# GpSimd issues the additions of an expert block ahead of the gathers for the block four later

## The chip, the core and the metric

The kernel runs on one core of a Trainium2 chip. The metric is the device time in microseconds (us) of one execution. The core's engines run on their own and meet at semaphores: PE (TensorE), DVE (VectorE), ACT (ScalarE), POOL (GpSimd) and SP (SyncE, which here only issues transfers). Sixteen DMA engines move data between the memory and the core for all of them.

## What is computed

One decoder layer on 1040 rows of 1024 numbers (16 meta tokens and 1024 tokens): an RG-LRU mixer, a layer norm, a mixture of experts, a layer norm. The change lies in the routed experts. Each row picks 8 of 64 experts; the reference gathers the rows of a block, runs one expert on them, weights the result and adds it to the rows that it came from:

```python
    def body(b, acc):
        rows = lax.dynamic_slice(row_tok, (b * EXPERT_BLOCK,), (EXPERT_BLOCK,))
        rw = lax.dynamic_slice(row_w, (b * EXPERT_BLOCK,), (EXPERT_BLOCK,))
        e = block_e[b]
        gu = x_pad[rows] @ w_gu[e]
        y = ((jax.nn.silu(gu[:, :f]) * gu[:, f:]) @ w_down[e]) * rw[:, None]
        return acc.at[rows].add(y)
```

A shared expert on all rows and the second layer norm follow.

## The kernel before

**Blocks.** Experts are sorted by the number of their rows. The kernel walks through 64 blocks in this execution, block t for one expert. Even blocks hold 164 rows, odd ones 128. A hardware loop runs 30 times over a pair (an even and an odd block), and four blocks follow it unrolled. `t = i + j` is the block, `b = j % 2` its parity, and every buffer of a block exists twice, one for each parity.

**What a block needs, engine by engine**, each engine in the order of its own program:

- SP loads the weights of the expert: two transfers of 1 MB (`wgu`, three blocks ahead) and one of 1 MB (`wd_raw`, two ahead).
- GpSimd issues the gathers, transfers that fetch rows by an index list: six of 128 KB for an even block, four for an odd one (`fetch`, L843), from `h1_rows` into `xg[b]`. It also issues the additions, transfers that add the block's result to `routed_rows` row by row (L874): two for an even block (128 and 36 rows), one for an odd one. All of them go through one software DMA queue.
- DVE in its step t: `wd_lo` of block t (L1414); `turn(t+2)`, which waits for the gathers of block t+2 and transposes `xg` into `xT` (L1372); `rows_from(t+4)`, the index list for the gathers of block t+4 (L1351); `hidden(t+1)` (L1382 to L1390); then the wait on `ysb_free`; `rows_of(t)`, which looks up the target rows and weights of block t (`picks`, L1357, to `to_row`, L1367) and stands right ahead of y; and its share of `y(t)`, the weighted result in `ysb[b]` (L1430, L1434).
- ACT in its step t: `wd_hi` of block t (L1136), the two `silu` of block t+1 (L1125), the wait on `ysb_free` and on `rows_of(t)`, and its share of `y(t)` (L1145, L1149).
- PE: `up(t+1)` (L996, needs `turn(t+1)`), then `down(t)` (L121 to L123, L1021, L1023; needs `wd_lo(t)` and `hidden(t)`).

**The order on GpSimd**, which the change touches. In its step t GpSimd first waits until `turn(t+2)` is done (`xT_ready`, so that `xg[b]` is free), waits for `rows_from(t+4)` inside `fetch`, and issues the gathers of block t+4. Then it waits until the additions of block t-1 have landed (`y_stored`), raises `ysb_free` (L868), which lets DVE and ACT make `y(t+1)`, waits for the two shares of `y(t)` (`y_act`, `y_dve`) and issues the additions of block t. Blocks 0 to 3 are gathered ahead of the loop.

Of the kernel before, what the change touches and what calls it, by code (L numbers as in the profile page):

```python
# [125 lines left out]
def build(nc, hT, h_rows, w_in, chan, w_gates, w_out, ln, router_w, router_b, w_gu, w_down,  # L126
# [534 lines left out]
    xg_clear, xT_ready = sem("xg_clear"), sem("xT_ready")  # L661
# [4 lines left out]
    def before(counts, i, j):  # L666


        return i * (sum(counts) // 2) + j // 2 * sum(counts) + j % 2 * counts[0]

    def stores_to(i, j):

        return loads(i, j) * STORES[j % 2] + 16 * (j % 2)
# [35 lines left out]
    sp_pass, pool_pass, pe_pass = sem("sp_pass"), sem("pool_pass"), sem("pe_pass")  # L709
# [13 lines left out]
    def steps(eng):  # L723

        n = eng.value_load(sched_i[0:1, 5:6], min_val=E - 4, max_val=T_MAX - 4)
        with eng.Fori(0, n, 2) as i:
            for b in range(2):
                yield i, b, 4
        for j in range(4):
            yield n, j, 3 - j  # L730

    with nc.Block() as block:  # L732
# [72 lines left out]
        @block.gpsimd  # L805
        def _(pool):

            s = Chain(pool, pool_step)
            s.n = pool_steps
            pool.memset(h1T[:, :, L:LP], 0.0).then_inc(z_clear, 1)  # L810
            pool.wait_ge(list_cleared, 16)

            def enlist(i):

                r = ROWS[i]
                pool.wait_ge(place_ready, i + 1)
                for j in range(TOP_K):
                    pool.indirect_dma_start(  # L818
                        out=expert_list,
                        out_offset=bass.IndirectOffsetOnAxis(ap=place[0:r, i, j:j + 1], axis=0),  # L820
                        in_=entry[0:r, i, j, :], in_offset=None).then_inc(listed, 16)

            for i in range(TILES - 2):
                enlist(i)

            pool.wait_ge(z_lo_ready, AHEAD + TILES)
            pool.wait_ge(norm_ready, TILES)
            for b in range(2):
                pool.memset(hid_hi[b][:, :, :].bitcast(F32), 0.0).then_inc(hid_clear, 1)
                pool.memset(hid_lo[b][:, :, :].bitcast(F32), 0.0).then_inc(hid_clear, 1)  # L830
                pool.memset(xg[b][:, :, :], 0.0).then_inc(xg_clear, 1)
            for i in range(TILES - 2, TILES):
                enlist(i)
            pool_n[0] = s.n


            def fetch(i, j):

                b = j % 2
                pool.wait_ge(from_ready, i + j + 1)  # L840
                pool.sem_inc(pool_pass, 1)
                for g in range(GB[b]):
                    pool.indirect_dma_start(  # L843
                        out=xg[b][:, g, :], out_offset=None, in_=h1_quarters,
                        in_offset=bass.IndirectOffsetOnAxis(ap=from_row[b][:, g:g + 1], axis=0),
                        bounds_check=NQ * L - 1, oob_is_err=False).then_inc(gathered[b], 16)

            pool.wait_ge(routed_cleared, 16)
            pool.wait_ge(routed_begun, 16 * TILES)
            pool.wait_ge(h1_stored, 16 * TILES)  # L850
            pool.wait_ge(xg_clear, 2)
            fetch(0, 0)
            fetch(0, 1)
            for j in range(2, 4):
                pool.wait_ge(xT_ready, j - 1)
                fetch(0, j)
            pool.wait_ge(sched_loaded, 16)
            for i, j, more in steps(pool):
                t, b = i + j, j % 2
                if more >= 4:  # L860
                    pool.wait_ge(xT_ready, t + 3)
                    pool.sem_inc(pool_pass, 1)
                    fetch(i, j + 4)

                pool.wait_ge(y_stored[1 - b], stores_to(i, j - 1))
                pool.sem_inc(ysb_free, 1)  # L868
                pool.wait_ge(y_act, t + 2)
                pool.sem_inc(pool_pass, 1)  # L870
                pool.wait_ge(y_dve, YS[1] + before(YS, i, j + 1))
                pool.sem_inc(pool_pass, 1)
                for half, r in enumerate((P, REST[b])[0:STORES[b]]):
                    pool.indirect_dma_start(  # L874
                        out=routed_rows,
                        out_offset=bass.IndirectOffsetOnAxis(ap=to_row[b][0:r, half:half + 1],
                                                             axis=0),
                        in_=ysb[b][0:r, half, :], in_offset=None,
                        bounds_check=L - 1, oob_is_err=False, compute_op=ALU.add
                        ).then_inc(y_stored[b], 16)  # L880

        @block.tensor
        def _(pe):
# [671 lines left out]
```

## Time and profile before

| | us |
|---|---|
| median of 3 runs | 1330.15 (1327.42 to 1332.71) |
| the profiled execution, its own time | 1323.39 |
| its span, first to last instruction | 1321.6 |
| PE busy in the span | 1223.2 (93%) |
| DVE busy | 825.8 (62%) |
| POOL busy | 661.9 (50%) |
| ACT busy | 431.8 (33%) |

A busy time is the sum of what an engine's instructions took, waits left out. The loop over the blocks fills the time from about 478 to 1270 us of the span; the mixer and the routing stand ahead of it, the last layer norm behind it. The median of the runs is 6.76 us above the profiled execution, whose rows are read below.

### The profile page before, as it was taken

The page shows a single profiled execution, that of the slowest core. Times are in us where ns is not written, and L with a number is a line of the kernel's source. Part 1 is how long each engine was busy: PE and PEld are TensorE (multiplying, and loading weights), DVE is VectorE, ACT ScalarE, POOL GpSimd, SP SyncE. Part 2 cuts the span into 40 slices and gives each one's busy share as a digit, 9 for nine tenths or more (in the row PEclk, how much of TensorE's full clock was granted, in tenths as well). Part 3 has the DMA queues.
Part 4 walks back from the last instruction along what each step waited for, and adds up shares of the span by engine and source line. Part 5 has one row for each costly group of instructions (what it writes and reads, how often), then busy time and mean ns, then how long its engine had stood idle before and what let it go on. Part 6 is the DMA issues. An engine that isn't in the chain of part 4 may idle for free. (4 is left out here: it accounts for less than half of the span.)

```text
span 1321.6 us, 23551 instructions
## 1 busy us (share of the span) xinstructions
PE 1223.2 (93%) x7492; PEld 1102.0 (83%) x7492; DVE 825.8 (62%) x1685; ACT 431.8 (33%) x597; POOL 661.9 (50%) x556
## 2 busy tenths in 40 slices
PE   7999999669898989999999999999999999999974
PEld 7999999647686668998899997999999899999831
DVE  7474839376887616655666664666566566656538
ACT  5352542713333012332333232333223332333223
POOL 6222211220665555665676667656666766657310
PEclk9999999889999989999999999999999999999987
DMA  7111110323242389999999999999999999999754
GB/s 274 49 48 33 48 49 17 127 76 125 97 130 70 97 247 382 363 346 358 350 344 371 350 356 317 347 342 359 340 350 359 314 370 345 318 376 334 225 127 170
DMA packets 86406, 320.39 MB, mean 242 GB/s; under 512 B 18144, under 2 KB 34581, under 8 KB 61409
## 3 DMA queue, kind: packets, MB, share of 16 engines
q1 hardware_dynamic: 56991, 250.68, 49.8%
q0 software_dynamic: 29072, 68.82, 21.1%
q10 hardware_dynamic: 306, 0.40, 0.1%
q8 instruction: 23, 0.38, 0.1%
q14 instruction: 14, 0.11, 0.0%
HBM read 278.71 MB, written 53.16 MB: 251 GB/s over the span
## 5 line engine op out<-in xcount | busy, mean ns | idle before, releaser
L996 PEld LDWEIGHTS bank<-xT,wgu 128*128 128x128 f32 x4096 | 524.4, 192 | 22.8 <-issue 15.3
L996 PE MATMUL bank<-xT,wgu 128*128 128x164 f32 (+1 forms) x4096 | 531.1, 290 | 11.7 <-issue 5.6
L843 POOL DMA_INDIRECT xg<-h_rows,from_row x320 | 353.4, 1104 | 123.3 <-issue 96.7
L874 POOL DMA_INDIRECT routed_rows<-ysb,to_row x96 | 150.9, 1572 | 190.6 <-issue 184.4
L1145 ACT ACTIVATE ysb<-bank,of_row 128x512 f32<-128x512 f32 x64 | 44.0, 687 | 418.9 <-issue 219.2
L1414 DVE TENSOR_TENSOR wd_lo<-wd_raw,wd_hi 128x1024 fp32r<-128x1024 f32 x128 | 151.2, 1223 | 43.9 <-ACT wd_hi L1136 21.6
L121 PE MATMUL bank<-hT_hi,win_hi 128*128 128x348 f32 x384 | 124.2, 324 | 9.6 <-DVE hT_lo L556 9.6
L1136 ACT ACTIVATE wd_hi<-wd_raw 128x1024 fp32r<-128x1024 f32 x128 | 127.9, 1048 | 1.4 <-issue 0.6
L122 PE MATMUL bank<-hT_lo,win_hi 128*128 128x348 f32 x384 | 124.0, 323 | 0.0
L123 PE MATMUL bank<-hT_hi,win_lo 128*128 128x348 f32 x384 | 123.5, 322 | 0.0
L818 POOL DMA_INDIRECT expert_list<-entry,place x72 | 74.2, 1030 | 89.7 <-DVE place L1253 69.9
L121 PE MATMUL bank<-wd_hi,hid_hi 128*128 128x512 f32 x256 | 108.2, 423 | 10.0 <-DVE wd_lo L1414 9.2
L369 POOL TENSOR_TENSOR win_lo<-win_raw,win_hi 128x1024 fp32r<-128x1024 f32 x16 | 40.9, 2559 | 147.8 <-ACT win_hi L473 147.8
L1372 DVE STREAM_TRANSPOSE xT<-xg 128x1536 f32<-128x1536 f32 x64 | 96.4, 1506 | 25.6 <-DMA xg<-h_rows,from_row 25.6
L122 PE MATMUL bank<-wd_lo,hid_hi 128*128 128x512 f32 x256 | 101.8, 398 | 0.6 <-issue 0.6
L123 PE MATMUL bank<-wd_hi,hid_lo 128*128 128x512 f32 x256 | 101.9, 398 | 0.2 <-issue 0.2
L1357 DVE TENSOR_TENSOR picks<-lists,pick 128x24 f32<-128x24 f32 x64 | 12.2, 190 | 134.0 <-POOLq L868 101.0
L121 PE MATMUL bank<-wout_hi,z_hi 128*128 128x512 f32 x144 | 61.3, 425 | 24.0 <-DVE z_lo L1163 12.6
L121 PEld LDWEIGHTS bank<-hT_hi,win_hi 128*128 128x128 f32 x384 | 72.8, 189 | 9.6 <-issue 9.6
L1125 ACT ACTIVATE gact<-bank 128x128 f32<-128x128 f32 (+1 forms) x128 | 34.8, 289 | 130.9 <-PE bank L996 86.1
L1382 DVE TENSOR_TENSOR hid<-gact,bank 128x128 f32<-128x128 f32 (+1 forms) x128 | 38.5, 301 | 55.8 <-PE bank L996 30.6
L122 PEld LDWEIGHTS bank<-hT_lo,win_hi 128*128 128x128 f32 x384 | 72.7, 189 | 0.0
(221 smaller groups left out, 1774.5 us busy)
## 6 DMA issues: line engine op xcount, KB each, us to landing
wgu<-in_w_gu SPq DMA_DIRECT2D x128, 1024.0 KB
wd_raw<-in_w_down SPq DMA_DIRECT2D x64, 1024.0 KB
win_raw<-in_w_in SPq DMA_DIRECT2D x16, 512.0 KB, 3.9
xg<-h_rows,from_row POOLq DMA_INDIRECT x320
hT_raw<-in_hT SPq DMA_DIRECT2D x8, 520.0 KB, 7.8
wout_raw<-in_w_out SPq DMA_DIRECT2D x1, 4096.0 KB, 12.8
h_in<-in_h_rows SPq DMA_DIRECT2D x8, 512.0 KB
h_rows<-h SPq DMA_DIRECT2D x8, 512.0 KB
```

The source lines that it names most:

```text
L121: pe.matmul(out, lhs[0], rhs[0], start=first, stop=False)
L122: pe.matmul(out, lhs[0], rhs[1], start=False, stop=False)
L123: return pe.matmul(out, lhs[1], rhs[0], start=False, stop=last)
L369: pool.tensor_tensor(win_lo[q % NW][:, :, :], win_raw[q % NW][:, :, :], win_hi[q % NW][:, :, :].bitcast(F32), ALU.subtract).then_inc(win_l ...
L818: pool.indirect_dma_start(out=expert_list, out_offset=bass.IndirectOffsetOnAxis(ap=place[0:r, i, j:j + 1], axis=0), in_=entry[0:r, i, j, : ...
L843: pool.indirect_dma_start(out=xg[b][:, g, :], out_offset=None, in_=h1_quarters, in_offset=bass.IndirectOffsetOnAxis(ap=from_row[b][:, g:g ...
L874: pool.indirect_dma_start(out=routed_rows, out_offset=bass.IndirectOffsetOnAxis(ap=to_row[b][0:r, half:half + 1], axis=0), in_=ysb[b][0:r, ...
L996: mm = pe.matmul(bank[:, 2 * f + half, 0:BLOCK[b]], wgu[b][:, f, k, c:c + P], xT[b][:, k, 0:BLOCK[b]], start=(k == 0), stop=(k == KT - 1))
L1136: act.activation(wd_hi[b][:, k, :], wd_raw[b][:, k, :], ACT.Copy).then_inc(wd_hi_ready, 1)
L1145: act.activation(ysb[b][:, 0, 0:512], bank[:, 4, :], ACT.Copy, scale=of_row[b][:, 0, 1:2]).then_inc(y_act, 1)
L1372: dve.transpose(xT[b][:, :, :].rearrange("p k (g a) -> p k g a", a=SQ), xg[b][:, :, :].rearrange("p g (k c) -> p k g c", c=SQ)).then_inc(x ...
L1414: dve.tensor_tensor(wd_lo[b][:, k, :], wd_raw[b][:, k, :], wd_hi[b][:, k, :].bitcast(F32), ALU.subtract).then_inc(wd_lo_ready, 1)
```

## The change

In GpSimd's step the lines that gather block t+4 move from the top of the step to its end. Nothing is added or removed; the waits inside the moved lines go along with them.

```diff
             for i, j, more in steps(pool):
                 t, b = i + j, j % 2
-                if more >= 4:
-                    pool.wait_ge(xT_ready, t + 3)
-                    pool.sem_inc(pool_pass, 1)
-                    fetch(i, j + 4)
                 pool.wait_ge(y_stored[1 - b], stores_to(i, j - 1))
                 pool.sem_inc(ysb_free, 1)
...
                         ).then_inc(y_stored[b], 16)
+                if more >= 4:
+                    pool.wait_ge(xT_ready, t + 3)
+                    pool.sem_inc(pool_pass, 1)
+                    fetch(i, j + 4)
```

## Rows read from the trace of the kernel before

**Rows 1.** Windows: busy us of each engine, granted clock, DMA share, GB/s.
```profile
478.00:1260.00 782.00, 762.94 (x5110) 708.52 (x5111) 475.13 (x1017) 240.56 (x383) 491.28 (x405) 0.99 1.00 341
```

**Rows 2.** Waits of DVE, 520 to 1250 us: total us, times, longest.
```profile
DVE picks L1357 <- POOLq L868: 98.3, 25, 7.2
...
DVE xT L1372 <- DMA xg<-h_rows,from_row: 5.8, 8, 1.1
```

**Rows 3.** Timeline of PE: start, us, line, operation, tiles, count, [idle before].
```profile
528.81 1.42 PE L996 MATMUL bank<-xT,wgu 128*128 128x164 f32 x9
...
552.32 0.86 PE L996 MATMUL bank<-xT,wgu 128*128 128x164 f32 x5
```

**Rows 4.** Timeline of DVE: turn(38), last of hidden(37), look-up of block 36.
```profile
935.36 1.77 DVE L1372 STREAM_TRANSPOSE xT<-xg 128x1536 f32<-128x1536 f32 x1
...
938.39 0.29 DVE L1387 TENSOR_TENSOR hid_lo<-hid,hid_hi 128x128 fp32r<-128x128 f32 x1
943.21 0.20 DVE L1357 TENSOR_TENSOR picks<-lists,pick 128x24 f32<-128x24 f32 x1 [4.53 <-POOLq L868]
```

**Rows 5.** Timeline of DVE: look-up and y of block 0, then turn(4).
```profile
505.79 0.20 DVE L1357 TENSOR_TENSOR picks<-lists,pick 128x24 f32<-128x24 f32 x1 [0.64 <-issue]
...
508.01 1.40 DVE L1434 SCALAR_TENSOR_TENSOR ysb<-bank,of_row,y_rest 36x512 f32<-36x512 f32 x2 [0.93 <-ACT y_rest L1149]
...
522.29 1.76 DVE L1372 STREAM_TRANSPOSE xT<-xg 128x1536 f32<-128x1536 f32 x1
```

**Rows 6.** Timeline of DVE: the end of y(26).
```profile
828.24 1.40 DVE L1434 SCALAR_TENSOR_TENSOR ysb<-bank,of_row,y_rest 36x512 f32<-36x512 f32 x2 [0.63 <-ACT y_rest L1149]
```

**Rows 7.** Timeline of POOL: the first addition of block 26.
```profile
830.52 2.09 POOL L874 DMA_INDIRECT routed_rows<-ysb,to_row  x1 [4.80 <-DVE ysb L1434]
```

**Rows 8.** Timeline of POOL: first and last gather of block 40, both additions of 36.
```profile
945.28 1.04 POOL L843 DMA_INDIRECT xg<-h_rows,from_row  x1 [0.30 <-issue]
...
952.11 1.00 POOL L843 DMA_INDIRECT xg<-h_rows,from_row  x1 [0.30 <-issue]
954.73 1.62 POOL L874 DMA_INDIRECT routed_rows<-ysb,to_row  x1 [1.62 <-issue]
956.66 1.44 POOL L874 DMA_INDIRECT routed_rows<-ysb,to_row  x1 [0.30 <-issue]
```

**Rows 9.** Timeline of POOL: the last gather of block 0, of block 8, of block 60.
```profile
473.80 1.01 POOL L843 DMA_INDIRECT xg<-h_rows,from_row  x1 [0.30 <-issue]
...
561.79 1.00 POOL L843 DMA_INDIRECT xg<-h_rows,from_row  x1 [0.30 <-issue]
...
1194.88 1.00 POOL L843 DMA_INDIRECT xg<-h_rows,from_row  x1 [0.30 <-issue]
```

**Rows 10.** Timeline of DVE: turn(0), turn(8), turn(60), turn(62).
```profile
476.03 1.78 DVE L1372 STREAM_TRANSPOSE xT<-xg 128x1536 f32<-128x1536 f32 x1 [9.15 <-DMA xg<-h_rows,from_row]
...
569.83 1.78 DVE L1372 STREAM_TRANSPOSE xT<-xg 128x1536 f32<-128x1536 f32 x1 [1.03 <-DMA xg<-h_rows,from_row]
...
1201.28 1.77 DVE L1372 STREAM_TRANSPOSE xT<-xg 128x1536 f32<-128x1536 f32 x1
...
1224.30 1.77 DVE L1372 STREAM_TRANSPOSE xT<-xg 128x1536 f32<-128x1536 f32 x1
```

**Rows 11.** Timeline of PE: up(62), then the first matmul of down(61) and of down(63).
```profile
1230.07 9.07 PE L996 MATMUL bank<-xT,wgu 128*128 128x164 f32 x64
1240.04 0.47 PE L121 MATMUL bank<-wd_hi,hid_hi 128*128 128x512 f32 x1 [0.90 <-DVE wd_lo L1414]
...
1259.29 0.77 PE L121 MATMUL bank<-wd_hi,hid_hi 128*128 128x512 f32 x1 [4.20 <-DVE wd_lo L1414]
```

**Rows 12.** Timeline of DVE: the end of y(62).
```profile
1256.16 1.40 DVE L1434 SCALAR_TENSOR_TENSOR ysb<-bank,of_row,y_rest 36x512 f32<-36x512 f32 x2 [0.91 <-ACT y_rest L1149]
```

**Rows 13.** Timeline of POOL: the first addition of block 62, the addition of block 63.
```profile
1261.19 1.56 POOL L874 DMA_INDIRECT routed_rows<-ysb,to_row  x1 [5.50 <-issue]
...
1268.82 1.57 POOL L874 DMA_INDIRECT routed_rows<-ysb,to_row  x1 [4.34 <-issue]
```

## The prediction

> **What bounds the kernel now.** I read the windows over the block loop first. From 478 to 1260 us PE is busy for 762.94 of 782.00 us at a granted clock of 0.99, and the DMA engines are busy all the time (share 1.00) [rows 1]. So PE has 19 us to win in the whole loop, and no more. Then PE's timeline: from the start of up(4) to the start of up(6) it needs 23.51 us for a pair of blocks without a gap [rows 3]. The loop as a whole takes a little more: turn(4) starts at 522.29 and turn(62) at 1224.30, which is 702.01 us for 29 pairs, 24.21 each [rows 5, 10]. PE and the DMA engines set the pace together, and the rest of the loop follows about as fast.
>
> Next I looked for who is late, in the waits of DVE. The largest is the look-up of a block waiting for GpSimd's release of ysb (L868): 98.3 us in 25 waits, up to 7.2 [rows 2]. The change takes hold right there: GpSimd issues six gathers for about 8 us [rows 8] and only then releases ysb. A reader who stops here expects a gain. But this wait ends on DVE, and PE has hardly an idle slot behind it; and the same view has a second row that matters more: eight times a turn waited for its gathers, 5.8 us in all [rows 2]. Those gathers were issued early, by the order which the change gives up. So I followed the gathers.
>
> **The change, part by part.** *Number of instructions.* None is added or removed. GpSimd already alternates additions and gathers; what changes is which gathers stand between two groups of additions. Before: additions of t-1, gathers of t+4, additions of t. After: additions of t-1, gathers of t+3, additions of t. The work of GpSimd for a pair is the same. What it is moved past: the wait for the landing of the additions of t-1, the release of ysb, and the waits for y(t). In the software DMA queue each group of gathers moves behind the additions of one more block. The queue of SP is not touched.
>
> *What the release of ysb gains: nothing that lasts.* The release for y(t+1) now stands behind the gathers of t+3 instead of those of t+4, again one group of gathers behind the additions of t-1, whose landing it waits for in any case. I put it at 0.
>
> *What the gathers lose.* This is the term. After the change the gathers of t+4 can't be issued before the additions of t, these not before y(t), and y(t) stands on DVE behind turn(t+2) in the same step. And turn(t+2) waits for the gathers of t+2. That closes a ring over one pair of blocks: landing of the gathers of t+2, turn(t+2), hidden(t+1), look-up and y(t), additions of t, gathers of t+4, their landing. Before, the gathers of t+4 only had to come behind the additions of t-1 and so y(t-1) and turn(t+1): the same ring had three blocks of time instead of two. I add the ring up for even t, which has more gathers and more additions:
>
> - turn(t+2) and hidden(t+1), from the start of the turn at 935.36 to the end of the last hidden instruction at 938.39 + 0.29: 3.32 us [rows 4].
> - The pause until the look-up begins where nothing holds it up: 0.64 [rows 5]. (In rows 4 it was 4.53, held by L868; in the ring ysb is free by then, since GpSimd stands waiting for y(t) behind its release.)
> - Look-up and y(t), 505.79 to 508.01 + 1.40: 3.62 [rows 5].
> - From the end of y to the first addition where GpSimd waits for it: 828.24 + 1.40 = 829.64 to 830.52, 0.88 [rows 6, 7].
> - Two additions, 954.73 to 956.66 + 1.44: 3.37, and 0.30 to the next instruction [rows 8].
> - Six gathers, 945.28 to 952.11 + 1.00: 7.83 [rows 8].
>
> The sum is 19.96 us without the landing of the last gather. The trace shows a landing only where a turn waits for it: block 8's came 569.83 - 562.79 = 7.04 us after the last issue ended, with the weights streaming beside it; block 0's came 476.03 - 474.81 = 1.22 us after it, ahead of the loop [rows 9, 10]. Where a turn didn't wait there is an upper bound: block 60's rows were there 1201.28 - 1195.88 = 5.40 us after [rows 9, 10]. So the bounds are 1.2 and 7.0. Most turns of the loop did not wait, so I take a value near the row of block 60, 5.6: a little above it, because the gathers now stand right behind two additions in their queue, and well below 7.0, because a slower loop asks less of the DMA engines. The ring is then 19.96 + 5.6 = 25.56 us, above PE's 23.51 and above today's 24.21. For odd t the ring has one addition less (954.73 to 956.66: 1.93 us) and two gathers less (a fifth of 945.28 to 952.11 each: 2.7 us), so it is shorter by over 4 us and does not bind [rows 8].
>
> The Trainium skill, "DMA: Bandwidth & Descriptors", section on the anatomy of one DMA on the SWDGE path, gives a fixed 2.0 us plus the bytes over 436 GB/s for a transfer issued by GpSimd; my estimate from it is 2.3 us for a gather of 128 KB. The trace agrees for block 0 (1.22 us, even less) and disagrees for block 8 (7.04 us). By the page the ring would be 22.3 us and would not bind at all.
>
> *The sum.* y(0) ends at 508.01 + 1.40 = 509.41 [rows 5]. The additions and gathers behind it and the landing take 0.88 + 3.37 + 0.30 + 7.83 + 5.6 = 17.98, so turn(4) starts at 527.4 instead of 522.29. 29 rings of 25.56 are 741.2 us, so turn(62) starts at 1268.6 instead of 1224.30 [rows 10]. Before, up(62) began at 1230.07, 4.0 us after that turn had ended at 1226.07 [rows 10, 11]; now PE waits at that place, so up(62) begins as the turn ends, at 1270.4: 40.3 us later. Behind it something is given back, since GpSimd is no longer late: the first addition of block 62 came 3.63 us after the end of y(62) (1257.56 to 1261.19), where 0.88 is needed, and PE's wait of 0.90 us ahead of down(61) goes too [rows 11 to 13]. That is 2.75 + 0.90 = 3.6 us. The change is +36.7 us. The profiled execution took 1323.39 us and would take 1360.1; on the median, 1330.15 + 36.7 = 1366.9, rounded to 1367.
>
> Each tenth of a microsecond of landing time is worth 3 us (30 landings on the way: those of blocks 4 to 62).
>
> *What PE's waits may add.* PE now waits 25.56 - 23.51 = 2.05 us in each pair, ahead of an even up. After a wait of 0.90 us the first matmul of a down took 0.47 us, after one of 4.20 us it took 0.77 [rows 11], so matmuls may run slower behind a long wait. A wait of 2 us lies between, and PE has those 2 us to spare for a slower stretch; I put it at 0 and keep it for the upper end.
>
> **Rivals.**
>
> *Faster: the gathers land early enough, and the earlier additions win.* If the ring falls under 24.2 us, GpSimd's old lateness (98.3 us of waits) can shrink, and PE's idle 19 us go at best: 1330 - 19 = 1311. The point is a mean landing time of 4.2 us (19.96 + 4.2 = 24.2). For it speaks that the ring itself thins the traffic and that idle engines landed a gather in 1.22 us; against it that DMA is busy for the whole loop and that eight turns waited even with gathers issued a block earlier. This is where the page's rule would lead.
>
> *No change: the landing takes about 4.2 to 4.6 us*, and the ring costs what today's lateness costs: 1330 within 7.
>
> *Much slower: the gathers queue behind the additions*, and the landing is block 8's 7.0 us or more: 1.4 us more for each of 30 landings is 42 us, so 1409 and above. Matmuls that run slower behind PE's waits would lead there too.
>
> *The change does nothing*, since GpSimd alternates anyway: that is the case of no change, and the shift by one block speaks against it.
>
> **Chances.** The forecast, a landing time of about 4.7 to 6.9 us, 1340 to 1406: 0.70. Faster 0.08. No change 0.12. Much slower 0.10. The predicted time is the forecast's, 1367. The range takes in half of the two neighbours: 1330 to 1412. A measurement of this kernel can tell about 0.5% (6.7 us) from no change: faster by more than that 0.08, within it 0.12, slower 0.80.
>
> **What would show it.** In the profile of the changed kernel: the starts of even turns stand about 25.6 us apart; even turns wait for the DMA of xg nearly every time, several us each, where eight waits of 1.1 at most stood; PE idles about 2 us in a pair ahead of an even up; the look-up no longer waits for L868 ahead of even blocks; GpSimd's first addition of an even block waits for DVE's y (L1434), not for issue. I am wrong if even turns don't wait for xg, or if GpSimd's additions still wait for the landing of the ones before. If turns wait but the pair takes under 24.5, the landing time was mis-sized.

## The result, and the profile after

The changed kernel takes 1416.64 us (median of 4 runs, 1414.59 to 1423.69), the kernel before 1331.43 beside it: 1.065 times as long, 95% interval 1.060 to 1.070, 85 us more. Forecast were 1367 us, with a range up to 1412. The sign and the ring came true, the size did not: 37 us were forecast. The profiled execution took 1415.9 us, its span 1414.1, against 1323.39 and 1321.6 before.

First the window over the block loop, 478 to 1352 us (columns: stretch, length, busy us and instructions of PE, weight loads, DVE, ACT, POOL, then granted clock, DMA share, GB/s), which answers [rows 1]:

```profile
478.00:1352.00 874.00, 798.48 (x5130) 732.99 (x5128) 478.13 (x1018) 245.33 (x383) 501.06 (x411) 0.97 0.93 306
```

PE is now idle for 76 us of the loop (874.00 - 798.48), and the DMA engines, busy throughout before, are idle for 7% of it on average. Neither sets the pace any more. Who does is in the waits, 520 to 1340 us (who waited for whom: us in total, times, longest):

```profile
ACT ysb L1144 <- DVE to_row L1366: 304.4, 44, 13.6
POOL routed_rows L869 <- DVE ysb L1433: 227.7, 31, 21.4
DVE xT L1371 <- DMA xg<-h_rows,from_row: 203.6, 31, 10.5
...
PE bank L995 <- DVE hid_lo L1386: 37.2, 9, 5.4
```

The look-up's wait for the release of ysb, the largest of DVE in [rows 2], is gone. In its place stands what the forecast named: the even turns wait for their gathers, all 30 of them and one odd turn, 203.6 us in 31 waits where [rows 2] had 5.8 in 8, and GpSimd waits for y, not y for GpSimd.

The ring can be read off one pair. Here it is for DVE, from turn(6) to turn(8), and for GpSimd between them (start, length; the wait ahead in brackets):

```profile
568.58 1.78 DVE L1371 STREAM_TRANSPOSE xT<-xg 128x1536 f32<-128x1536 f32 x1 [10.13 <-DMA xg<-h_rows,from_row]
...
571.62 0.29 DVE L1386 TENSOR_TENSOR hid_lo<-hid,hid_hi 128x128 fp32r<-128x128 f32 x1
572.55 0.20 DVE L1356 TENSOR_TENSOR picks<-lists,pick 128x24 f32<-128x24 f32 x1 [0.64 <-issue]
...
574.77 1.40 DVE L1433 SCALAR_TENSOR_TENSOR ysb<-bank,of_row,y_rest 36x512 f32<-36x512 f32 x2 [0.92 <-ACT y_rest L1148]
...
594.43 1.78 DVE L1371 STREAM_TRANSPOSE xT<-xg 128x1536 f32<-128x1536 f32 x1 [6.16 <-DMA xg<-h_rows,from_row]
```

```profile
577.05 2.09 POOL L869 DMA_INDIRECT routed_rows<-ysb,to_row  x1 [7.18 <-DVE ysb L1433]
579.45 1.44 POOL L869 DMA_INDIRECT routed_rows<-ysb,to_row  x1 [0.30 <-issue]
581.19 1.09 POOL L843 DMA_INDIRECT xg<-h_rows,from_row  x1 [0.30 <-issue]
...
588.32 1.00 POOL L843 DMA_INDIRECT xg<-h_rows,from_row  x1 [0.30 <-issue]
```

Turn and hidden 3.33 (to 571.91), pause 0.64, look-up and y 3.62 (to 576.17), 0.88 to the first addition, two additions 3.84 (to 580.89), 0.30, six gathers 8.13 (to 589.32), landing 5.11: 25.85 us, with nothing left over. That is near the forecast of 25.56. But the mean is not: turn(4) starts at 538.01 and turn(62) at 1322.58, 784.57 us for 29 pairs, 27.05 each, where [rows 5, 10] gave 24.21.

The whole difference of the two spans, 92.5 us, divides so: 6.3 us before turn(0), where nothing was changed (482.4 against [rows 10]); 9.4 from turn(0) to turn(4) (forecast 5.1); 82.6 in the 29 pairs (forecast 39.2); and 5.8 given back behind turn(62) (forecast 7.6: the slack of 4.0 and the tail of 3.6). In a second profile of the changed kernel, turn(0) starts at 476.67, turn(4) at 529.61 and turn(62) at 1315.0, so turn(0) comes 0.6 us later than before, the stretch from turn(0) to turn(4) is 6.7 us longer, and the pair takes 27.08. The miss is the pair, in both.

### The profile page after: what moved, and what is told of

Read it like the earlier page. It is cut to its first block and busy times, and to the rows that moved or that the text cites. A ratio compares the mean times of both kernels' runs of the same rounds, so it can differ in the third digit from the quotient of the medians.

```text
span 1414.1 us, 23551 instructions
## 1 busy us (share of the span) xinstructions
PE 1262.2 (89%) x7492; PEld 1130.7 (80%) x7492; DVE 828.1 (59%) x1685; ACT 436.5 (31%) x597; POOL 667.0 (47%) x556
## 5 line engine op out<-in xcount | busy, mean ns | idle before, releaser
L995 PE MATMUL bank<-xT,wgu 128*128 128x164 f32 (+1 forms) x4096 | 559.5, 297 | 67.6 <-DVE hid_lo L1386 37.2
L995 PEld LDWEIGHTS bank<-xT,wgu 128*128 128x128 f32 x4096 | 546.0, 197 | 87.2 <-DVE hid_lo L1386 41.4
L843 POOL DMA_INDIRECT xg<-h_rows,from_row x320 | 344.5, 1077 | 110.8 <-issue 96.7
L869 POOL DMA_INDIRECT routed_rows<-ysb,to_row x96 | 164.9, 1718 | 281.0 <-DVE ysb L1433 235.5
L123 PEld LDWEIGHTS bank<-hT_hi,win_lo 128*128 128x128 f32 x384 | 72.9, 190 | 0.0
```

The source lines that it names most:

```text
L123: return pe.matmul(out, lhs[1], rhs[0], start=False, stop=last)
L843: pool.indirect_dma_start(out=xg[b][:, g, :], out_offset=None, in_=h1_quarters, in_offset=bass.IndirectOffsetOnAxis(ap=from_row[b][:, g:g ...
L869: pool.indirect_dma_start(out=routed_rows, out_offset=bass.IndirectOffsetOnAxis(ap=to_row[b][0:r, half:half + 1], axis=0), in_=ysb[b][0:r, ...
L995: mm = pe.matmul(bank[:, 2 * f + half, 0:BLOCK[b]], wgu[b][:, f, k, c:c + P], xT[b][:, k, 0:BLOCK[b]], start=(k == 0), stop=(k == KT - 1))
```

## The experiments

The theory (the ring): the pace is the sum of the steps from one even turn's gathers to the next, and whatever stands in that chain costs its own length in each of 29 pairs. The rivals: the order in the software queue (gathers behind additions land late), and throughput (PE, DVE or the DMA engines are simply slower, and the wait for the gathers only shows it).

### How many gathers stand behind the additions

Four kernels issue the first gathers of block t+4 at the top of the step, as before, and the others behind the additions, as in the change. `first` is (1, 0), (2, 1), (3, 2) and (4, 3) for even and odd blocks; the kernel before is (6, 4), the changed one (0, 0). `fetch` takes the slice of the gathers to issue as a third argument, which isn't shown.

```diff
+                first = (1, 0)[b]
+                if more >= 4 and first:
+                    pool.wait_ge(xT_ready, t + 3)
+                    pool.sem_inc(pool_pass, 1)
+                    fetch(i, j + 4, slice(None, first))
...
                         ).then_inc(y_stored[b], 16)
+                if more >= 4:
+                    if not first:
+                        pool.wait_ge(xT_ready, t + 3)
+                        pool.sem_inc(pool_pass, 1)
+                    fetch(i, j + 4, slice(first or None, None))
```

Expected of (1, 0):

> One of the six gathers of an even block goes ahead of the additions (odd block: none), the rest stay behind them. Ring theory (gathers of t+4 behind y(t) behind turn(t+2) behind gathers of t+2): a pair took 27.05 us in the changed kernel, and each gather that goes ahead takes its 8.29 / 6 = 1.38 us out of the ring, so 25.7 a pair and 1417 - 29 x 1.38 = 1377 us. Queue theory (gathers land late because they stand behind additions in the DMA queue): the loss of 85 us goes with the share of gathers that stand behind, 9 of 10, so about 1408 us.

Of (2, 1):

> Two of the six gathers of an even block and one of four of an odd block go ahead of the additions. Ring theory: 27.05 - 2 x 1.38 = 24.3 us a pair, about what the kernel before takes (24.2), so about 1335 us. Queue theory: 7 of 10 gathers still stand behind additions, 1331 + 0.7 x 85 = 1391 us.

Of (3, 2):

> Three of six and two of four gathers go ahead of the additions. Ring theory: the ring is 22.9 us and binds no more; the time is that of the kernel before, 1331, or up to 10 us less, since ysb is released behind five gathers instead of six ahead of an even block. Queue theory: half of the gathers stand behind additions, 1331 + 0.5 x 85 = 1374 us.

Of (4, 3):

> Four of six and three of four gathers ahead of the additions, two and one behind. Ring theory: the ring is 21.5 us and is far from binding, so the time is that of the run with three and two ahead, 0.994 of the kernel before, within 0.4%. Queue theory: a third of the gathers still behind additions, slower than the kernel before by 25 us.

| ahead | us | ratio to before (95%) | turn(4), turn(62) | us per pair |
|---|---|---|---|---|
| 0, 0 (the change) | 1416.64 | 1.065 (1.060 to 1.070) | 538.0, 1322.6 | 27.05 |
| 1, 0 | 1365.67 | 1.026 (1.021 to 1.030) | 534.8, 1272.6 | 25.44 |
| 2, 1 | 1342.90 | 1.006 (1.001 to 1.012) | 534.5, 1243.6 | 24.45 |
| 3, 2 | 1324.35 | 0.994 (0.992 to 0.997) | 530.1, 1229.8 | 24.13 |
| 4, 3 | 1331.25 | 0.999 (0.996 to 1.003) | 527.1, 1238.1 | 24.52 |
| 6, 4 (before) | 1331 | 1 | 522.3, 1224.3 | 24.21 |

One even gather taken out of the chain (1.00 + 0.30 us) takes 1.6 us off the pair, the second 1.0, the third 0.3 (with the second and the third, an odd gather moves too). So the curve falls as the ring says and flattens where the ring comes down to the other bound. The queue rival in the form that was forecast, a loss in proportion to the gathers behind additions, is out: it wanted 1408, 1391 and 1374 us for the first three. With (3, 2) the kernel is 0.6% faster than before, by one comparison; with (4, 3) there is no difference. The last was forecast at 0.994 within 0.4%: a small miss.

The waits of (3, 2), 520 to 1250 us:

```profile
POOL routed_rows L873 <- issue: 157.8, 87, 7.9
DVE xT L1376 <- DMA xg<-h_rows,from_row: 154.2, 57, 5.9
```

GpSimd's waits are no longer put down to y, and the turns wait briefly, even and odd (57 times, 2.7 us on average where the changed kernel has 6.6). PE is busy for 717.50 us of that window, at a granted clock of 1.00.

### The same order, written in another place

The program order of before, gathers at the top of the step, but for block t+3: the gathers then stand behind the same additions as in the change, in another place of the loop's text.

```diff
-            for j in range(2, 4):
+            for j in range(2, 3):
...
-                if more >= 4:
-                    pool.wait_ge(xT_ready, t + 3)
+                if more >= 3:
+                    pool.wait_ge(xT_ready, t + 2)
                     pool.sem_inc(pool_pass, 1)
-                    fetch(i, j + 4)
+                    fetch(i, j + 3)
```

> The program order of the kernel before, gathers at the top of the step, but for the block three later instead of four, so that GpSimd issues the same sequence of gathers and additions as the changed kernel. Ring theory: only the distance counts, so about 1417 us, the time of the changed kernel. Place theory (the loss comes from where the release of ysb and the waits for y stand in the step): about 1331 us, the time of the kernel before.

Measured: 1412.72 us, ratio 1.060 (1.055 to 1.065), turn(4) at 529.0 and turn(62) at 1322.4, 27.36 a pair. That is the changed kernel's time, as it should be: but for the ends of the loop, GpSimd runs the same instructions and waits in the same order in both. So where the lines stand in the step is nothing, only the order counts. What it is about the order that costs, the ring or the place in the queue, this run can't tell; the others do.

### Delays on GpSimd, inside and outside the ring

First, four register reads between the additions and the gathers of even blocks, and the same reads ahead of the wait for y, where GpSimd is idle.

```diff
                         ).then_inc(y_stored[b], 16)
+                for _ in range(0 if b else 4):
+                    blocks_to_run(pool)
                 if more >= 4:
```

> The changed kernel, and for even blocks GpSimd reads a register from the schedule four times between the additions and the gathers behind them, some 1.5 to 3 us in which it issues nothing. Ring theory: this stands in the ring, so each us costs 29 us, 44 to 87 in all: 1460 to 1504. Throughput theory (GpSimd has too much to do in a pair): the same.

> The changed kernel, and the same four reads for even blocks between the release of ysb and the wait for y, where GpSimd waited for y 7.3 us on average (227.7 us in 31 waits). Ring theory: they disappear in that wait, 1417 us within 7. Throughput theory: GpSimd has as much to do as with the reads behind the additions, so 1460 to 1504.

Measured: 1388.67 us (1.048, 1.044 to 1.052) and 1391.67 (1.051, 1.047 to 1.055). No difference, and the first is no test, since the reads did not delay the gathers, where 1.5 to 3 us had been expected. The gap behind the additions stayed what it was (909.65 to 909.96), 0.31 us on average over 29 pairs. Both ratios are also 0.014 to 0.017 below the changed kernel's 1.065, which was not forecast; it comes up again below.

```profile
908.21 1.44 POOL L869 DMA_INDIRECT routed_rows<-ysb,to_row  x1 [0.30 <-issue]
909.96 1.08 POOL L843 DMA_INDIRECT xg<-h_rows,from_row  x1 [0.30 <-issue]
```

Then eight short fills of an unused tile (`scratch`, with a semaphore of its own) on GpSimd in the same two places, in every block.

```diff
+                pool.wait_ge(scratch_done, t * 8 + 1)
+                pool.sem_inc(pool_pass, 1)
+                for n in range(8):
+                    pool.memset(scratch[:, n, :], 0.0).then_inc(scratch_done, 1)
```

> The changed kernel with eight short memsets of unused space on GpSimd between the additions and the gathers of every block, about 0.15 us each with the pause behind it, 1.2 us in all. (Register reads in this place, tried before, ran on beside the additions and held nothing up.) Ring theory: 1.2 us more in the ring of even blocks, 29 x 1.2 = 35 us above the changed kernel. Throughput theory (GpSimd's work of a pair sets the pace): 29 x 2.4 = 70 us above.

> The same eight memsets behind the release of ysb, ahead of the wait for y. Ring theory: ahead of an even block they run while GpSimd waits for y anyway, so within 7 us of the changed kernel. Throughput theory: 70 us above it, as in the run with the memsets behind the additions.

Beside them, the changed kernel once more:

> The changed kernel once more, on the chip on which the next runs are timed: as before 1.050 to 1.065 of the kernel before.

Measured: 1401.66 (1.048, 1.040 to 1.056), 1398.22 (1.050, 1.044 to 1.055), and the changed kernel 1412.40 (1.060, 1.053 to 1.067). The fills took 1.03 us, but began beside the second addition, which ends at 949.53:

```profile
948.10 1.43 POOL L872 DMA_INDIRECT routed_rows<-ysb,to_row  x1 [0.30 <-issue]
949.05 1.03 POOL L882 MEMSET scratch<- 128x30 f32 x8
950.24 1.08 POOL L845 DMA_INDIRECT xg<-h_rows,from_row  x1 [0.16 <-issue]
```

The gap grew from 0.30 to 0.71, so the ring would ask for 0.41 x 29 = 12 us; 3 us more by the medians and 2 less by the ratios were measured against the same fills outside the ring, which can't be told from 0 or from 12. They rule out only that GpSimd's throughput is the bound: then both would have come out slower than the changed kernel, and both came out a little faster.

### Delays on DVE, inside and outside the ring

DVE's rows stand one behind the other, so a delay can't hide here: 24 fills of such a tile ahead of the look-up of even blocks (in the ring), and of odd blocks (outside; there `b == 1`).

```diff
                 dve.wait_ge(ysb_free, t + 1)
                 dve.sem_inc(dve_pass, 1)
+                if b == 0:
+                    dve.wait_ge(scratch_done, t * 12 + 1)
+                    for n in range(24):
+                        dve.memset(scratch[:, n, :], 0.0).then_inc(scratch_done, 1)
                 rows_of(i, j)
```

> The changed kernel with 24 short fills of an unused tile on DVE, ahead of the look-up of every even block (about 0.07 us each by the fill of the tile small in the profile, so 1.6 us by estimate). These stand in the ring: behind hidden(t+1), ahead of the look-up and y(t). The ring theory: every pair is longer by what they take, 29 x 1.6 = 46 us over the kernel with the same fills ahead of odd blocks. The rival, that the pace is set by the DMA queue or by PE's slower stretches and the gathers only seem to be a chain: DVE is idle for almost half of the time, so the same time as with the fills ahead of odd blocks, within 10 us.

> The same fills ahead of the look-up of every odd block, which the ring does not bind. The ring theory: odd blocks have about 4 us to spare (one addition and two gathers less), so the time of the changed kernel (ratio 1.05 to 1.065) within 10 us, and some 46 us less than with the fills ahead of even blocks. The rival (DVE's or PE's time is what counts): the same time as with the fills ahead of even blocks.

Measured: 1436.91 us (1.082, 1.076 to 1.088) in the ring, 1387.40 (1.045, 1.040 to 1.050) outside it. From the trace of the first:

```profile
947.22 0.29 DVE L1388 TENSOR_TENSOR hid_lo<-hid,hid_hi 128x128 fp32r<-128x128 f32 x1
947.46 0.71 DVE L1433 MEMSET scratch<- 128x10 f32 x24
948.90 0.20 DVE L1358 TENSOR_TENSOR picks<-lists,pick 128x24 f32<-128x24 f32 x1 [0.73 <-issue]
```

The fills were shorter than estimated: the pause of 0.64 us became 1.39 (947.51 to 948.90), 0.75 more, so the ring asks for 22 us over the changed kernel. Against the changed kernel's ratios of 1.060 and 1.065 the difference is 0.017 to 0.022 of 1331, 22 to 29 us. The profiled execution, the fastest of the four, shows less: 27.42 us a pair, 0.35 over the changed kernel's two profiles, so 10 us: the pause is 0.75 us longer in every pair, but the other terms of the ring came out 0.4 shorter in sum. The same work on the same engine, one block later, made nothing slower. DVE's throughput is out, and the fills count in the ring and not outside it.

Not expected was that the fills outside made the kernel faster than the changed one, by 1.5 to 2%. Its pairs took 25.66 us (turn(4) 536.5, turn(62) 1280.6). Of the 49 us between the two kernels the fills in the ring explain 22 at most; the others are this gain.

### Time taken out of the ring

The wait for ysb and the look-up of even blocks move ahead of turn(t+2), into the time when DVE waits for the gathers.

```diff
+                if b == 0:
+                    dve.wait_ge(ysb_free, t + 1)
+                    dve.sem_inc(dve_pass, 1)
+                    rows_of(i, j)
                 if more >= 2:
                     dve.wait_ge(up_done, t * UPS + 2 * UPS)
                     turn(i, j + 2)
...
-                dve.wait_ge(ysb_free, t + 1)
-                dve.sem_inc(dve_pass, 1)
-                rows_of(i, j)
+                if b == 1:
+                    dve.wait_ge(ysb_free, t + 1)
+                    dve.sem_inc(dve_pass, 1)
+                    rows_of(i, j)
```

> The changed kernel with the wait for ysb and the look-up of even blocks moved ahead of turn(t+2), where DVE waits for the gathers anyway. It takes the pause of 0.64 us and the look-up out of the ring, and ACT's share of y can run beside hidden(t+1): from the end of hidden to the end of y about 2.5 us in the place of 4.3. The ring theory: 1.8 us less in each pair, 29 x 1.8 = 52 us less than the changed kernel, ratio to the kernel before about 1.02. The rival (the pace is set by the queue of gathers or by PE): the landing takes up what is won, and the time is that of the changed kernel within 10 us, ratio 1.05 or more.

Measured: 1375.89 us, ratio 1.032 (1.026 to 1.037), 26.12 a pair (turn(4) 529.0, turn(62) 1286.4). That is 37 us under the second measurement of the changed kernel, where 52 were expected. Throughput and the queue would have left it where it was. Why not 52 shows on DVE, in one pair:

```profile
944.66 0.29 DVE L1386 TENSOR_TENSOR hid_lo<-hid,hid_hi 128x128 fp32r<-128x128 f32 x1
946.02 0.75 DVE L1434 TENSOR_SCALAR ysb<-bank,of_row 128x512 f32<-128x512 f32 x1 [1.07 <-PE bank L123]
947.20 1.40 DVE L1438 SCALAR_TENSOR_TENSOR ysb<-bank,of_row,y_rest 36x512 f32<-36x512 f32 x2 [0.42 <-ACT y_rest L1148]
```

With the look-up out of the way, y stands waiting 1.07 us for PE's down. It does so in 13 of the 29 pairs, for 0.5 to 4.8 us, and from the end of hidden to the end of y it takes 3.0 us on average where 2.5 were expected (4.3 in the changed kernel). So PE's work between two turns is a second branch of the ring, and in these pairs it was only a little shorter than the one that was cut.

The same move with (3, 2) gathers ahead, where the ring should bind no longer:

> The same move of the look-up in the kernel that issues 3 of 6 (even) and 2 of 4 (odd) gathers ahead of the additions and the rest behind them. That kernel took 24.13 us for a pair where PE needs 23.5. The ring theory: its ring becomes shorter than PE's own time, so up to 0.6 us less in each pair, 17 us: ratio to the kernel before 0.982 to 0.994. The rival (PE and the DMA engines hold that kernel, not the ring): no change, 0.994 within 0.004.

Measured: 1330.87 us, 0.999 (0.996 to 1.002). No gain, and above both forecasts (0.982 to 0.994 and 0.990 to 0.998); it looks 0.5% worse than (3, 2) without the move, but the two intervals overlap. That kernel is not held by the look-up.

### What the landing is made of

The loop loads one eighth of the up weights only (the rest of `wgu` keeps old data, so the result of the experts is another one), in the changed kernel and in the kernel before. The matmuls are all there.

```diff
-            def load_wgu(i, j, f):
+            def load_wgu(i, j, f, n=KT):
...
-                    load_wgu(i, j + 3, f)
+                    load_wgu(i, j + 3, f, 1)
```

> The changed kernel without seven eighths of the up weights in the loop: from block 3 on each transfer of wgu brings one of eight slices and the rest stays from the first blocks, so the result is not the reference's. 1.75 of 3 MB of weights for a block are gone, all instructions of the engines stay. Ring theory with the landing as the part that the weights' traffic sets: the landing falls from 5.5 to about 2.5 us, the ring to 24.1 us a pair, 1417 - 29 x 3 = 1330 us. If the landing is set by the two additions ahead of the gathers in the queue: it stays, 1417 us.

> The kernel before with the same part of the up weights left out. PE's own 23.5 us a pair are then all that is left: the 19 us of PE's waits in the loop go, about 1311 us, and the changed kernel without those weights is slower than this by at most 20 us (ring theory) or by 85 to 106 us (if the landing is set by the additions).

Measured: 1342.09 us (1.012, 1.007 to 1.016) for the changed one and 1304.62 (0.985, 0.981 to 0.989) for before. In the first, GpSimd's last gather and the turn that waits for it:

```profile
904.11 0.99 POOL L843 DMA_INDIRECT xg<-h_rows,from_row  x1 [0.30 <-issue]
```

```profile
906.85 1.78 DVE L1371 STREAM_TRANSPOSE xT<-xg 128x1536 f32<-128x1536 f32 x1 [4.09 <-DMA xg<-h_rows,from_row]
```

The landing is 906.85 - 905.10 = 1.75 us, and 2.40 on average over 29 pairs (1.1 to 3.6), though the gathers stand behind the same two additions. So most of the 5.6 us of the changed kernel is the weights' traffic, not the queue behind additions; that rival had wanted 85 to 106 us between the two kernels. It is 35 by the ratios, more than the ring's 20 at most: the kernel before came down to PE's own 23.54 us a pair (522.0 to 1204.6), the changed one to 24.86 (527.3 to 1248.3), though its ring, with a landing of 2.40 and turn and hidden at 3.32, would be 23.2, no longer than PE's time. The trace shows which term grew: turn and hidden take 4.72 us on average (3.3 to 7.9), where the changed kernel has 3.78. Hidden(t+1) needs the odd block's up as well as the turn, and the two chains, of nearly one length, hold each other up there. That they cost more than the longer of them is what these means show; why hidden is late in one pair and not in the next is not shown.

The Trainium skill, "DMA: Bandwidth & Descriptors", section on the anatomy of one DMA on the SWDGE path, gives 2.0 us plus the bytes over 436 GB/s, by estimate 2.3 us for 128 KB. These two kernels show when that agrees: 2.40 us on average here, and 5.11 in the pair above, with the weights streaming beside it.

## Why the prediction was right about the sign and wrong about the size

The step that failed is the adding up of the ring. Its chain was right, but three of its terms were taken too short: additions 3.37 us (measured 3.84), gathers 7.83 (8.29), turn and hidden 3.32 (3.76, since hidden itself waits in ten of 28 pairs, which the prediction had at nothing). With the smaller differences that made a pair of 27.05 us where 25.56 were forecast.

**What bounds, which wait ends and which begins, the ring, odd blocks not binding:** right. Also right, by the waits: the release of ysb brought nothing that lasts, and the cover of PE (19 us) was all there was to win. One link was off, at no cost to the ring: by the program an even up also waits for the first half of hidden, whose banks it overwrites, and so begins behind that and not as its turn ends, as forecast. For example, up(14) begins at 682.85, where turn(14) ended at 681.97 and that half at 682.79. That is the wait of PE for hid_lo in the view of waits above.

**Landing, 5.6 us:** right on the mean, by luck in part, and wrong on its form. From the end of the last gather's issue to the turn it is 5.48 us on average in the 28 pairs from turn(6) on, but about 5 in 22 of them (4.2 to 5.4), and 6.6 to 9.0 in six. With the first pair's 9.09 the mean of 29 is 5.60. But one of the two reasons for the value, the place behind two additions, is what the run with an eighth of the up weights speaks against, and in the second profile the mean is 5.13.

**The additions, 3.37 us.** The prediction took the first addition from [rows 8], 1.62 us, where GpSimd had not waited for y. In the ring GpSimd always waits for y, and for that case [rows 7], which the same prediction used for the 0.88 us, already had 2.09. Measured: 2.09 and 1.44, 3.84 in nearly every pair. 0.47 x 29 = 14 us.

**The gathers, 7.83 us.** [rows 8] is a group in which a gather took 1.07 us on average (a fifth of 945.28 to 952.11, less the pause of 0.30). The mean over all gathers was there to be read. On the pages, of before and then of after (busy us, mean ns of one | idle before):

```profile
L843 POOL DMA_INDIRECT xg<-h_rows,from_row x320 | 353.4, 1104 | 123.3 <-issue 96.7
```

```profile
L843 POOL DMA_INDIRECT xg<-h_rows,from_row x320 | 344.5, 1077 | 110.8 <-issue 96.7
L869 POOL DMA_INDIRECT routed_rows<-ysb,to_row x96 | 164.9, 1718 | 281.0 <-DVE ysb L1433 235.5
```

By the mean of before, six gathers and five pauses are 6 x 1.104 + 5 x 0.30 = 8.12 us. Measured are 8.29 on average. 0.46 x 29 = 13 us.

**Turn and hidden, 3.32 us, and "I put it at 0" for PE behind its waits.** In 18 of the 28 pairs it is 3.3 us. In the ten others it is 4.0 to 5.3, since the second half of hidden(t+1) waits: for ACT's second silu of the odd block, which by the program waits for PE's up of that block alone. So in the pair of turn(38), where the last hidden ends at 1001.50, 5.34 us behind the start of its turn:

```profile
996.16 1.78 DVE L1371 STREAM_TRANSPOSE xT<-xg 128x1536 f32<-128x1536 f32 x1 [5.28 <-DMA xg<-h_rows,from_row]
...
1000.69 0.29 DVE L1381 TENSOR_TENSOR hid<-gact,bank 128x128 f32<-128x128 f32 x1 [1.92 <-ACT gact L1124]
...
1001.21 0.29 DVE L1386 TENSOR_TENSOR hid_lo<-hid,hid_hi 128x128 fp32r<-128x128 f32 x1
```

The window view of PE in those microseconds (columns as above):

```profile
992.50:996.00 3.50, 2.05 (x10) 1.44 (x11) 0.00 (x0) 0.00 (x0) 2.89 (x3) 1.00 0.94 247
996.00:1000.00 4.00, 1.52 (x7) 0.98 (x7) 2.57 (x5) 0.00 (x0) 2.53 (x3) 1.00 0.88 214
1000.00:1005.00 5.00, 4.85 (x15) 3.81 (x15) 1.41 (x7) 0.96 (x2) 0.00 (x0) 0.66 0.97 365
```

PE was busy for only 3.57 of 7.5 us, waiting for no one that the trace shows, at a granted clock of 1.00. Only behind that, when hidden was nearly done, did the clock stand at 0.66 on average, between its two levels of 1.2 and 2.4 GHz; y, which then waited 2.16 us for PE, felt it. In the loop the clock is 0.97, against 0.99 in [rows 1]. Nor is this pair like the others: in the pair of turn(8) PE was busy without a gap at a granted clock of 1.00, the last matmul on record of up(9) ends at 592.10, and the silu starts only at 594.59. In all ten it starts 0.7 to 3.8 us behind that matmul, in nine of them released by what the trace calls remote. The ends of matmuls are modelled, so PE may be later than its rows; what holds the silu is not shown. The clock does not: between the two silu it was 1.00 in nine of the ten. The mean over the pairs is 0.44 us more for the turn and hidden and 0.11 for y and the pause behind it, 0.55 x 29 = 16 us. The prediction named slower matmuls behind PE's waits and put their price at 0, with the argument that PE has 2 us a pair to spare; but a late up, if that is what it is, costs more than PE's own chain: it holds hidden, which stands in the ring.

**The sum.** 0.47 + 0.46 + 0.44 + 0.11 - 0.12 (landing) = 1.36 of the 1.49 us by which the pair was missed. The rest is the first pair, 538.01 to 568.58, which these means leave out: 30.6 us, 3.6 over the mean of the others, is 0.13 for each of 29.

In the second profile the miss is as large and lies otherwise: over its 29 pairs the additions are 0.48 over the forecast, the gathers 0.28, turn and hidden 0.86, y and the pause behind it 0.37, and the landing 0.47 under it, together 1.52. So the additions' share holds; how the rest divides between hidden, gathers and landing changes from one execution to the next.

The first pair shows the long landing. Block 6's last gather ended its issue at 559.49, and its turn started at 568.58, 9.09 us later. What moved in the pair, and then in the next one (568.5 to 594; packets, MB and share of the hardware queue, which carries the weights):

```profile
DMA packets 1907, 10.35 MB, mean 339 GB/s; under 512 B 369, under 2 KB 369, under 8 KB 916
...
q1 hardware_dynamic: 1104, 8.12, 70.5%
```

```profile
DMA packets 1491, 6.92 MB, mean 272 GB/s; under 512 B 346, under 2 KB 346, under 8 KB 946
...
q1 hardware_dynamic: 625, 4.46, 47.5%
```

8.12 MB of weights in one pair and 4.46 in the next, where a pair needs 6.3. The seven pairs with a landing over 6 us moved 7.7 to 8.3 MB, the other 22 moved 4.3 to 7.7. The reading: once PE waits, the buffers of the weights come free in bunches, the DMA engines stand idle in one pair and are crowded in the next, and a gather in the crowded one lands late. That the two go together is shown, that the bunching is the cause is argued (a longer pair also has more time for weights). In the kernel before the DMA engines were busy all the time.

**The rivals.** "Faster" and "no change" needed a landing of 4.6 us or less: it was 5.0 in most pairs. "Much slower" (1409 and above) is where the time fell, but not for the reasons it named: the gathers' queueing behind additions the runs exclude, and of the slower matmuls behind PE's waits only the late hidden, 16 us, may be an effect. The time came from terms of the forecast that were each a little short, all on the same side, since each had been read from an instance in which nothing stood in the way.

**Still open.** Why the two kernels with fills on GpSimd, the two with register reads and the one with fills on DVE's odd side are all 1 to 2% faster than the changed kernel. On the odd side the pairs took 25.66 us and ranged from 24.2 to 26.9 where those of the changed kernel range from 24.5 to 30.7, so it is the long pairs that are missing there. Term by term, its landing took 4.67 us on average (5.60 in the changed kernel), its gathers 7.65 (8.28), turn and hidden 3.37 (3.78), while GpSimd stood 1.62 us between y and the first addition (0.93). So a delay outside the ring shortened terms inside it, and a sum of fixed terms doesn't foresee that; how was not taken apart. Different chips measured the groups of kernels, so across groups the ratios to the kernel before are what counts.

## What to carry to other kernels

When a transfer is moved behind a step, write down the ring that it closes (who waits for it, what that one does, until the transfer can be issued again) and the number of blocks that the ring spans. Here one block more of delay took the ring from three blocks to two, and with it the slack; with half of the gathers left in their place the slack stayed. Take each term of such a ring from the mean of its group, or from an instance with the wait that it will have in the ring; here the clean instances made three terms short, and the errors didn't cancel but added up, times the number of rounds. And where two chains of nearly the same length run side by side, as PE's and the ring's do, cutting one (as in the look-up moved ahead) gains only down to the other.

## What the runs showed of the hardware that was not expected

- GpSimd's own work ran beside the issue of its transfers: four register reads lengthened the gap between an addition and a gather by nothing (0.31 us on average), and 1.03 us of fills by 0.41.
- An addition of 128 rows took GpSimd 2.09 us where it had just waited for DVE's y, 1.62 where it had not ([rows 7, 8] and the changed kernel); the second one 1.44 in either case.
- The last gather of a block, 128 KB, landed 2.4 us on average after its issue with an eighth of the up weights, 5.1 in a common pair with all, and 9.1 in the pair that carried 8.12 MB of weights.
- 24 fills of 128 x 10 numbers took DVE 0.71 us, 0.03 each, less than half of the 0.07 that the estimate took from the fills of another tile.
